# Feed-forward and output projections with the tokens stationary and 512 weight columns moving, residual and norms token-major

## What is computed

```python
def rms_norm(x, g, eps=1e-6):
    xf = x.astype(jnp.float32)
    y = xf * lax.rsqrt(jnp.mean(xf * xf, axis=-1, keepdims=True) + eps)
    return (y * g.astype(jnp.float32)).astype(x.dtype)
...
def swiglu(h, w_gate, w_up, w_down):
    return (jax.nn.silu(h @ w_gate) * (h @ w_up)) @ w_down
```

## Time and profile before

| | |
|---|---|
| three runs | 2719.0, 2720.65, 2723.92 us; median 2720.65 |
| profiled execution | span 2725.8 us |
| TensorE busy | 2528.6 us (93%), 20780 recorded products |
| VectorE, ScalarE busy | 1707.1 us (63%), 1248.6 us (46%) |
| granted TensorE clock, mean | 0.966 |
| weight traffic | 480 MB, mean 176 GB/s |

### The profile page before, as it was taken

How to read it: one execution, slowest core, us unless ns; L and a number is a source line. 1 busy time by engine, 2 the same in 40 slices (tenths; PEclk the granted TensorE clock), 3 DMA queues, 4 the chain that set the end, 5 groups by cost and what they waited for, 6 DMA issues and landing times.

```text
span 2725.8 us, 48854 instructions
## 1 busy us (share of the span) xinstructions
PE 2528.6 (93%) x20780; PEld 2395.9 (88%) x20780; DVE 1707.1 (63%) x2804; ACT 1248.6 (46%) x1697; POOL 1.2 (0%) x6
## 2 busy tenths in 40 slices
PE   6799997999999999999888998999999999887998
PEld 5689996888998999999887898999999999756997
DVE  6565574656766565566767576577655557646655
ACT  4443453444544444445445554455444345435443
POOL 0000000000000000000000000000000000000000
PEclk9899999999999999999898999999999999888999
DMA  6456656533555665544351344555545555363453
GB/s 218 181 200 242 241 203 229 189 109 124 186 202 216 236 226 196 211 147 154 132 174 52 120 171 154 185 175 173 179 170 179 180 177 183 114 215 137 170 178 116
DMA packets 71591, 480.14 MB, mean 176 GB/s; under 512 B 8784, under 2 KB 9296, under 8 KB 17744
## 3 DMA queue, kind: packets, MB, share of 16 engines
q1 hardware_dynamic: 66240, 468.74, 48.8%
q10 hardware_dynamic: 5136, 8.28, 1.0%
HBM read 471.48 MB, written 1.05 MB: 173 GB/s over the span
## 4 chain that ended last, share of the span: by engine, by line
PE 73%; DVE 13%; ACT 7%; DMA 4%; issue 3%; ACTq 0%; DVEq 0%
PE bank L264 64%; ACT whi L223 4%; DVE wlo L243 2%; DMA raw<-w_main 2%; DVE wlo L230 2%; PE bank L1115 2%; DMA raw<-w_down 1%; PE bank L997 1%; PE bank L935 1%; DVE ARX L686 1%; DVE HX L637 1%; DVE tmpx L631 1%; PE bank L985 1%; PE bank L553 0%; PE bank L1639 0%
## 5 line engine op out<-in xcount | busy, mean ns | idle before, releaser
L264 PE MATMUL bank<-HNX_hi,whi 128*128 128x256 f32 x2968 | 866.2, 293 | 64.3 <-DVE wlo L243 24.4
L223 ACT ACTIVATE whi<-raw 128x2048 fp32r<-128x2048 f32 (+1 forms) x378 | 705.5, 1868 | 334.6 <-PE bank L264 149.4
L264 PE MATMUL bank<-HNX_hi,wlo 128*128 128x256 f32 x2968 | 849.8, 287 | 0.0
L264 PE MATMUL bank<-HNX_lo,whi 128*128 128x256 f32 x2968 | 834.6, 286 | 0.0
L230 DVE TENSOR_TENSOR wlo<-raw,whi 128x1024 fp32r<-128x1024 f32 (+1 forms) x378 | 453.4, 1199 | 570.1 <-ACT whi L223 569.5
L264 PEld LDWEIGHTS bank<-HNX_hi,whi 128*128 128x128 f32 x2968 | 582.4, 196 | 91.7 <-issue 50.7
L264 PEld LDWEIGHTS bank<-HNX_hi,wlo 128*128 128x128 f32 x2968 | 583.1, 196 | 0.0
L264 PEld LDWEIGHTS bank<-HNX_lo,whi 128*128 128x128 f32 x2968 | 573.2, 196 | 1.1 <-issue 0.9
L243 DVE TENSOR_TENSOR wlo<-raw,whi 128x1024 fp32r<-128x1024 f32 (+1 forms) x378 | 450.8, 1193 | 0.0
L264 PE MATMUL bank<-HNC_hi,whi 128*128 128x256 f32 x1344 | 390.2, 290 | 11.6 <-DVE tmpc L448 4.5
L264 PE MATMUL bank<-HNC_lo,whi 128*128 128x256 f32 x1344 | 381.7, 284 | 0.0
(11 more groups left out here) (349 smaller groups left out, 2923.7 us busy)
## 6 DMA issues: line engine op xcount, KB each, us to landing
raw<-w_main SPq DMA_DIRECT2D x270, 1024.0 KB, 4.8
raw<-w_ada SPq DMA_DIRECT2D x72, 1024.0 KB, 4.8
raw<-w_down SPq DMA_DIRECT2D x72, 1024.0 KB, 4.9
raw<-w_down SPq DMA_DIRECT2D x36, 768.0 KB, 4.2
raw<-w_cmp SPq DMA_DIRECT2D x4, 1024.0 KB, 4.8
tmpx<-ARX ACTq DMA_DIRECT2D x18, 128.0 KB, 4.8
tmpx<-ARX ACTq DMA_DIRECT2D x32, 64.0 KB, 4.7
HX<-x_in SPq DMA_DIRECT2D x2, 512.0 KB, 6.0
```

The source lines that it names most:

```text
L223: NS.activation(WHI[q % HIS][:, 0:size], RAW[m % SLOTS][:, 0:size], ACT.Copy).then_inc(sems["w_hi"], 1)
L264: return NT.matmul(dst, (WHI[ordinal[n] % HIS], WLO[n % SLOTS])[w][:, k * 2 * P + col:k * 2 * P + col + P], x[xp][:, kx, :], start=start, ...
```

## The change

**Layout.** The residual `HX[P, 2, 1024]` is token-major: token 128i+p at [p, i, :]. Inputs and output are stored that way in memory.

**Products.** For gate and up, the way down and the output projections, the stationary operand is a slice of 128 features x 128 tokens of the activations, and the moving one 512 columns of weights. The projections into the mixers stay as they were. The weights are laid out anew: a gate and up block holds four slices of 128 features with 256 gate columns and 256 up columns beside each other, so that two blocks make a pair; the blocks for the way down hold two slices of 1024 columns, read by `w_down[f][:, k0:k1, c0:c1]`. There are 24 products of 512 columns to a block in place of 48 of 256.

```diff
+            def rows(n, parts, width, x, ks, start, stop, waits=None, order=None):
...
+                def one(t, h, bank):
+                    if start:
+                        on(pe, free.get(bank.name))
+                    tok = slice(t * P, (t + 1) * P)
+                    for j, (k, kx) in enumerate(ks):
+                        if on(pe, *(waits or {}).get(kx, ())):
+                            at = k * width + h * HALF
+                            hi, lo = (w[:, at:at + HALF] for w in (WHI[ordinal[n] % HIS], WLO[n % SLOTS]))
+                            NT.matmul(bank[:, :], x[0][:, kx, tok], hi, start=start and j == 0, stop=False)
+                            NT.matmul(bank[:, :], x[0][:, kx, tok], lo, start=False, stop=False)
+                            mm = NT.matmul(bank[:, :], x[1][:, kx, tok], hi, start=False, stop=stop and j == len(ks) - 1)
+                    return mm if pe else None
+
+                def emit(m):
+                    half = len(parts) // 2
+                    for part in parts[m * half:(m + 1) * half]:
+                        mm = one(*part)
+                    return mm
+                return emit
```

```diff
+                def silu(p, n):
...
+                    tmp = S.TMP[p % 2].rearrange("p (t c) -> p t c", t=2)
+                    th, read, ud = up(f"{t}_tanh"), up(f"{t}_gate_read"), up(f"{t}_up_done")
+                    if on(act, done(n), held.get(("turned", p % 2))):
+                        NS.activation(tmp, gate, ACT.Tanh, scale=0.5).then_inc(th.sem, 1)
+                    if on(dve, th):
+                        NV.scalar_tensor_tensor(tmp, tmp, 1.0, gate, ADD, MUL).then_inc(read.sem, 1)
+                        dve.wait_ge(*read)
+                        NV.scalar_tensor_tensor(tmp, tmp, 0.5, up_, MUL, MUL).then_inc(ud.sem, 1)
+                    free[BANK[a].name] = free[BANK[b].name] = ud
+                    later(S, 2, lambda: turn_pair(p, tmp, ud))
+
+                def turn_pair(p, tmp, ud):
...
+                    turned, hi, lo = up("pe_step"), up(f"{t}_g_hi"), up(f"{t}_g_lo")
+                    bank, kt = BANK[6 if S.lag and kept_bank[0] else 4], 2 * p % 8 if S.chunked else 2 * p
+                    if on(pe, ud, free.get(bank.name)):
+                        for f in range(2):
+                            for c in range(2):
+                                mm = NT.transpose(bank[:, (2 * f + c) * P:(2 * f + c + 1) * P], tmp[:, c, f * P:(f + 1) * P], ident)
+                        mm.then_inc(turned.sem, 1)
+                    g = [x[:, kt:kt + 2, :].rearrange("p a b -> p (a b)") for x in S.G]
+                    if on(act, turned, down_done):
+                        NS.activation(g[0], bank[:, :], ACT.Copy).then_inc(hi.sem, 1)
+                    if on(dve, hi):
+                        NV.tensor_tensor(g[1], bank[:, :], g[0].bitcast(fp32), SUB).then_inc(lo.sem, 1)
+                    free[bank.name] = lo
+                    held["turned", p % 2] = turned
```

```diff
+            def load_gain(S, spec):
+
+                t, loaded = S.tag, up(f"{S.tag}_in_gb", 16)
+                if spec[0] == "ada":
+                    src, written = GATES[3 * spec[1] + spec[2], S.seq].rearrange("k p -> (k p)"), gates_written[spec[1:]]
...
+                    src, written = A["post_rows"][spec[1]], None
+                if on(act, written, free.get((t, "gb"))):
+                    act.dma_start(S.GB[:, :], bass.AP(tensor=src.tensor, offset=src.offset, ap=[[0, P], [1, D]])).then_inc(loaded.sem, 16)
+                return loaded
...
+                    gates_written[L, j] = up("gate_out", 32)
+                    if on(act, made):
+                        for q in range(2):
+                            act.dma_start(GATES[3 * L + j, q].rearrange("k p -> p k"), GA[:, at + q:at + 2 * KD:2], allow_slow_non_contiguous=True).then_inc(sems["gate_out"], 16)
```

```diff
+                def squares_of_y(i):
+
...
+                    junk_free(0, ("sqy", i, 0))
+                    if act:
+                        act.wait_ge(*y[0][i])
+                        NS.activation(S.JUNK[:, 0:HALF], a[:, :], ACT.Square, accum_out=SQA[:, i:i + 1]).then_inc(keys[0][0], 1)
+                    if on(dve, y[0][i], y[1]):
+                        NV.tensor_tensor(S.Y[:, i, HALF:D], b[:, :], S.GB[:, HALF:D], MUL).then_inc(keys[1][0], 1)
+                    junk_free(1, ("sqy", i, 1))
+                    if act:
+                        act.wait_ge(*m["yg", i, 1])
+                        NS.activation(S.JUNK[:, HALF:D], b[:, :], ACT.Square, accum_out=SQB[:, i:i + 1]).then_inc(keys[0][1], 1)
+                    if dve:
+                        dve.wait_ge(*m["sqy", i, 0])
+                        NV.tensor_tensor(S.Y[:, i, 0:HALF], a[:, :], S.GB[:, 0:HALF], MUL).then_inc(keys[1][1], 1)
+                    free[a.name], free[b.name] = m["yg", i, 0], m["sqy", i, 1]
+                    free[t, "gb"] = m["yg", i, 0]
...
+                def add_back(i):
+                    for h, cols in parts:
+                        sem = mark(("h", i, h), "resid")
+                        if dve:
+                            dve.wait_ge(*m["ry", i])
+                            dve.wait_ge(*m["yg", i, h])
+                            NV.scalar_tensor_tensor(S.H[:, i, cols], S.Y[:, i, cols], RSTD[:, i:i + 1], S.H[:, i, cols], MUL, ADD).then_inc(sem, 1)
...
+                def shrink(i):
+                    for h, cols in parts:
+                        sem = mark(("s", i, h), "shrunk")
+                        if on(dve, m["rh", i], *free.get((t, "dst"), ())):
+                            NV.tensor_scalar(S.Y[:, i, cols], S.H[:, i, cols], RSTDH[:, i:i + 1], None, MUL).then_inc(sem, 1)
+
+                def turn_and_split(i):
+                    gain, shift = pre
+                    banks = (BANK[6], BANK[7]) if S.chunked else (BANK[2 - 2 * i], BANK[3 - 2 * i])
+                    tok = slice(i * P, (i + 1) * P)
+                    for h, bank in enumerate(banks):
+                        turned, no = up("pe_step"), mark(("no", i, h), "normed")
+                        if on(pe, m["s", i, h], free.get(bank.name)):
+                            for k in range(4):
+                                mm = NT.transpose(bank[:, k * P:(k + 1) * P], S.Y[:, i, h * HALF + k * P:h * HALF + (k + 1) * P], ident)
+                            mm.then_inc(turned.sem, 1)
+                        if on(act, turned, *(mod if (i, h) == (0, 0) else ())):
+                            for k in range(4):
+                                dst, src = S.Y[:, i, h * HALF + k * P:h * HALF + (k + 1) * P], bank[:, k * P:(k + 1) * P]
+                                if shift is None:
+                                    op = NS.activation(dst, src, ACT.Copy, scale=gain(4 * h + k))
+                                else:
+                                    op = NS.activation(dst, src, ACT.Identity, bias=shift(4 * h + k), scale=gain(4 * h + k))
+                            op.then_inc(no, 1)
+                        free[bank.name] = m["no", i, h]
+                    for h in range(2):
+                        s1, s2 = mark(("hi", i, h), "hn_hi"), mark(("lo", i, h), "hn_lo")
+                        hi, lo = (S.HN[w][:, 4 * h:4 * h + 4, tok] for w in range(2))
+                        if dve:
+                            dve.wait_ge(*m["no", i, h])
+                            src = S.Y[:, i, h * HALF:(h + 1) * HALF].rearrange("p (k q) -> p k q", k=4)
+                            NV.tensor_copy(hi, src).then_inc(s1, 1)
+                            dve.wait_ge(*m["hi", i, h])
+                            NV.tensor_tensor(lo, src, hi.bitcast(fp32), SUB).then_inc(s2, 1)
+
```

The order of `norm()` for lane X, and the first blocks of a feed-forward layer behind it:

```diff
+                if t == "x":
+                    if y:
                         table_of(ACT.Sqrt)
...
-                        tot_h = add_up(S, S.HG, sum_h, N4, now(f"{t}_hg_sum"))
-                        reads.append(tot_h)
-                    free[t, "sums"] = reads
+                        squares_of_y(0)
+                        inverse(0, SQA, SQB, ROOT, RSTD, "sqy", "by", "ry")
+                        add_back(0)
+                        if pre:
+                            squares_of_h(0)
+                        squares_of_y(1)
+                        if pre:
+                            inverse(0, SHA, SHB, ROOTH, RSTDH, "sqh", "bh", "rh")
+                            shrink(0)
+                        inverse(1, SQA, SQB, ROOT, RSTD, "sqy", "by", "ry")
+                        add_back(1)
+                        if not pre:
+                            return [[m["h", i, h] for h in range(2)] for i in range(2)]
+                    else:
+                        squares_of_h(0)
...
+                    yield ("L", 3.0)
...
+                    turn_and_split(0)
+                    squares_of_h(1)
+                    inverse(1, SHA, SHB, ROOTH, RSTDH, "sqh", "bh", "rh")
+                    if then is not None:
+                        table_of(then)
...
```

(17 more changed lines are left out.)

767 lines of the change are left out of this document (352 added, 415 removed).

## The result

The changed kernel takes 2773.8 us (median of four runs, 2771.9 to 2777.8), the kernel before 2722.0 us (2719.0 to 2723.9): 1.0195 times as long, interval 1.0181 to 1.021. 2640 us were predicted, with a range up to 2710. The profiled span is 2770.3 us.

The account below looks back on a forecast made before the run. Dense stages were taken as bound by how many products TensorE starts and how far apart. Terms -162 - 25 + 73 + 30 - 7 + 10 = -81 us took the profiled 2725.8 to 2645, stated as 2640 us; range 2575 to 2710.

Parts of the forecast that it names:

- Step 1: Feed-forward and output projections: 7608 products of 512 columns replace 15216 of 256, 23 ns saved each; -162 us after deductions.
- Rival (c): On TensorE, the 12.8 ns are a fixed cost of each product: 99 us won instead of 175, 2715 us; chance 0.07.
- Step 2: Work that leaves TensorE: 45 groups of sums and 28 spreading products, -25 us.
- Step 3: New transposes on TensorE, 396 for the pairs and 240 for the norms, in 159 groups of four: +73 us.
- Step 4: TensorE's waits at the norms of lanes X and C, whose chains have less work put in: +30 us.
- Step 5: The end, from the last product to the end of the span: some 7 us instead of 14.6, -7 us.
- Covered: Silu, VectorE and ScalarE work, weight traffic and small gain stores stay hidden; +10 us added in case this fails.
- The clock: Few of the replaced products run at half clock, where both forms cost the same: 3 us back.
- (d): TensorE's waits at new transposes and norms two to three times those taken (80 and 20 us): 2700 us; chance 0.11.
- (e): Columns themselves take 0.467 ns, so the wide products give nothing: +81 us, 2800 us; chance 0.06.
- (f): In TensorE's queue 159 transpose groups each hold the products behind them; at 0.9 us each 2780 us; chance 0.04.
- (g): Transposes reading fresh results don't overlap and cost 0.27 us each: 172 us for 73, 2740 us; chance 0.02.

Follow-up runs that it names:

- e2: Changed kernel with each product of 512 moving columns issued as two of 256: 2854.6 us, 80.8 us more than the changed kernel.
- e13: Rows of 64 unread products of several types after the changed kernel's last result; at 512 columns bf16 starts 216 ns apart, plain float32 passes 429 ns.
- e1: Rows of 64 unread float32r products of several widths after the changed kernel's last result: starts 226.7 ns apart at 512 columns, 173.8 at 384, 119.8 at 256.
- e5: Changed kernel with gains turned on TensorE and stored as rows (6 stores) instead of 12 stores of single floats: 2758.2 us, 15.6 us less.
- e8: Changed kernel with the context lane's silu done for each bank as soon as it is complete, not for both after the second block: 2744.0 us, 29.8 us less.
- e10: Changed kernel with e5, e8 and e9 together: 2704.1 us, 69.7 us less than the changed kernel, ratio 0.9926 to the kernel before.
- e3: Changed kernel without the 396 transposes of the gated activations (values wrongly laid out): 2710.6 us, 63.2 us less.
- e9: Changed kernel with VectorE's second half of the next weights' low part put ahead of the due jobs: 2759.3 us, 14.5 us less.
- e6: Kernel before with only the 12 stores of 1024 single floats added, read by nothing: 2749.8 us, 27.6 us more than the kernel before.
- e14: Changed kernel without the 240 transposes of the norms (values wrongly laid out): 2766.0 us, 7.8 us less.

## Why the prediction was wrong, step by step

- **Step 1, -162 us: mis-sized, the largest error.** The step that failed is "I take 213 + 3 = 216 ns": in the changed kernel products of 512 columns start 227 ns apart, which the prediction itself had named as a sign of being wrong. The term was 7608 x 23 ns = 175 us, 162 after two deductions, and it measured 81 (e2). It read the 12.8 ns of the earlier trace rows as a load that shows and took the width's cost from plain float32 passes, a type that lacks the cost (e13). Rival (c) named the fixed cost and gave it 0.07, because it is absent at half clock. It is absent there in the changed kernel too (427 ns, rows below), and at the full clock it is still there at 256, 384 and 512 columns (e1).

```profile
2575.02 0.63 PE L326 MATMUL psum<-wlo,HNX_hi 128*128 128x512 f32 x1
2575.45 0.63 PE L327 MATMUL psum<-whi,HNX_lo 128*128 128x512 f32 x1
```

- **Step 2, -25 us** was not measured by itself. The busy time of TensorE agrees with it: by estimate 98 us less for the products (7608 x 12.9 ns, 2 x 119.8 - 226.7), 25 less by this step, 69 more for 636 transposes at 108 ns and 24 more for the clock are -30, and the pages show -30.
- **Step 3, +73 us: right in sum by luck.** The 396 took 63 us with their waits, for 46; the 240 took 8, for 27. Together 71.
- **Step 4, +30 us: too much, by 12 us in the waits.** TensorE's idle time at lane X's norms, added up place by place in both timelines, is 48 us before and 70 after, 22 more where 20 were forecast. At lane C's norms it is 8 before and 4 after, where 10 more were forecast. The norm without filling was to win 2 us; it takes 12.4 (2562.1 to 2574.46 us) for 11.8. The chain begins behind a rounding of weights and a table load, which the count had left out, and at 2051 us it held a bank of the other lane, whose eviction stands behind the norm on ScalarE, for 7.7 us.
- **Step 5, -7 us: right.** The last product starts at 2763.04 us and the span ends 7.3 us later.
- **Covered, +10 us: failed in three places.** "The small stores of gains lie hundreds of us ahead of their readers" asked who reads them, not what they hold up: 15.6 us (e5). "Silu's chain of a pair (...) has two half blocks, 5.2 us, before its transposes" is nearly true of the transposes (12.4 us of waiting), but the banks have none in the context lane: 29.8 us (e8). And the low part of weights stood behind the transposed activations: 14.5 us (e9).
- **The clock** had 3 us, for products that cost the same in both forms. That the time at half clock might grow had no term; by the estimate above it is 24 us. In these kernels it goes with TensorE's idle time (idle 176, 202 and 255 us, at half clock 185, 211 and 244, in the kernel before, e10 and the changed kernel), so the gains of e8 and e10 contain a part of it and it is not added again below.

The misses add up: 81 (step 1) + 69.7 for the three waits together (e10) - 10 (allowed for) - 2 (step 3) - 12 (step 4) = 127 us more; 2774 - 2640 = 134. Part of e3's waits may be those of e8 and e9, and with these taken one by one (59.9 us) the sum is 117, so it is good to some 10 us and its closeness is partly luck. e10, in which the three waits are mended, is a second trial: 2640 - 10 + 81 - 2 - 12 = 2697 us, and it takes 2704.

Of the rivals, (c) came, with waits of the size of (d) on top. But (d) put them at the norms and the new transposes, and most were at silu's banks and at the weights. By the chances of (e), (f) and (g) slower than before had 0.12, not the 0.11 stated, and faster 0.85; nothing hangs on this.

## What to carry to other kernels

Take the price of an instruction from its own type: a row of another type, however like in width, can lack a fixed cost, and a cost for each product is found from two widths. When an output takes more columns, count banks before products: who may start writing while the last result is read? Give idle time a price at the clock too: where a kernel waits more, compare its mean granted clock. And for each new small transfer or eviction ask what waits behind it in its queue, not only when its reader comes.

## What was not expected of the hardware

- float32r products with a 128 x 128 stationary operand cost 13.3 ns each beyond their columns at the full clock, bf16 products and passes of plain float32 about 2.5 (e1, e13); at half clock nothing is added. With a stationary operand of 64 columns 17 ns are added at 512 moving columns and 7 at 256 (e1). Why isn't known.
- Two stores of 1024 single floats, 8 KB in all, delayed weight loads of 1 MB from 4.9 us to between 12 and 15, and twelve cost the kernel before 27.6 us (e6).
- 240 transposes cost 7.8 us, 396 others 63 (e14, e3): what one costs is set by what waits for it.
